# Chunked inverses of an RWKV layer: odd heads written across partition halves, and the series taken by powers

## The chip, the cores and the metric

The kernel runs on one core of one Trainium2 chip. The metric is the device time of one execution in microseconds (us). Besides the trace of one profiled execution there are three timed runs.

## The reference

A transformer of three layers over 512 tokens of width 1024: a window-attention layer, a grouped-attention layer, and a hybrid layer that adds the outputs of a sparse attention and of an RWKV-7 recurrence. The change touches the recurrence alone:

```
def rwkv7_step(state, inp):
    r_t, w_t, k_t, v_t, kk_t, a_t = inp
    sa = jnp.einsum('bhvk,bhk->bhv', state, -kk_t)
    state = (state * w_t[:, :, None, :] + sa[..., None] * (kk_t * a_t)[:, :, None, :]
             + v_t[..., None] * k_t[:, :, None, :])
    y = jnp.einsum('bhvk,bhk->bhv', state, r_t)
    return state, y
```

It has 8 heads of 64 keys by 64 values. After the scan come a group norm, a bonus term, a gate, and the product with `w_out`, whose second half of rows belongs to the recurrence and whose first half to the attention.

## The kernel before

The recurrence isn't stepped token by token. The 512 tokens are 4 tiles of 128 (index `i`), and each tile holds two chunks of 64 tokens: chunk 0 on partitions 0 to 63, chunk 1 on 64 to 127. For each head and chunk the kernel needs the inverse of a 64 x 64 triangular matrix of 1 minus A, where A is made of `grams` (products of the scaled keys) under masks. A is cut in two: its blocks of 16 x 16 on the diagonal (`mA`, and transposed `mD`) and the rest (`mE`). The near part is inverted by a series, then the far part by another series over it. Each step of a series is one **product**: for all 8 heads and both chunks, 16 matmuls of 64 x 64 by 64 x 64 in fp32 (each is two records in the trace). The names are A2, D2, Q2, D4, Z1, Z2, Z3 (near), QT (a transpose), KT, Y1_, Y2_ and RR (far), and X (values). RR is the inverse; `solved` multiplies it into values and decayed keys (HG), `state_maps`, `state_adds`, `own_outputs`, `state_step` and `state_outputs` carry the state, and `mean_job`, `square_job`, `spread_job` are the group norm.

TensorE (PE) writes each job to one of 8 PSUM banks in turn (`begin`), and can't begin a job before the one 8 before it has been copied out. Of one product, chunk 0 goes from partitions 0 to 63 into PSUM partitions 0 to 63, and chunk 1 from 64 to 127 into 64 to 127:

```
for h in range(8):
    for cs in halves_c:
        ins = mm(b[cs, h * CH:h * CH + CH], left[cs, h, :], right[cs, h, :], True, True)
```

So a product uses two of the four 64 x 64 quarters of the array. ScalarE (ACT) or VectorE (DVE) takes it out of PSUM (`move`, `plus`; `plus` adds the identity or the sum so far), and the next product waits for that. Between dependent products the program puts other work by hand, above all pieces of the output product (`out_part`: matmuls of 128 x 128 by 128 x 512, fp32), one at a time.

All orders are written out by hand: PE, ACT, DVE, GpSimd (POOL) and SyncE (SP) each run their own list, and meet at semaphores. In iteration `i` PE does the grams of tile `i` and the inverses of tile `i`, with the state work of tile `i-1` in between. Tile 0 has no earlier tile, and more `out_part` pieces beside it. After tile 3 a tail of state work and output products remains.

At the end of POOL's list stand a wait for four loads and one DMA issue:

```
pool.wait_ge(S("R_ar"), 16)
for i in range(NT):
    pool.wait_ge(s_x[i], 32)
pool.dma_start(gb2[:, :], ...).then_inc(s_gb[1], 16)
```

`s_x[i]` reaches 32 when `x_kept[i]`, the residual stream of tile `i` that was put out to HBM earlier, is back in SBUF (`x_out`). SP issues these four loads one after the other when the last projection of the recurrence is done. `gb2` is the row of final gains. On DVE only the additions to `x_out` (`add_half`) wait for `s_x[i]`, each for its own tile.

Of the kernel before, what the change touches and what calls it, by code (L numbers as in the profile page):

```python
# [25 lines left out]
F32 = mybir.dt.float32  # L26
# [80 lines left out]
def program(nc, A, out):  # L107
    ctx = ExitStack()
    with ctx:
# [30 lines left out]
        bank = [ctx.enter_context(nc.psum_tensor(f"bank{b}", [P, 512], F32)) for b in range(NBANK)]  # L140
# [157 lines left out]
        order, slot, J, who, nth, count = [], {}, {}, {}, {}, {"a": 0, "v": 0}  # L298
# [131 lines left out]
        mixB = hT[:, :, :].rearrange("p (j h) t -> p j h t", h=2)[:, :, 0, :]  # L430
        PC = stat[:, 544:576].rearrange("p (j c) -> p j c", j=4)
# [22 lines left out]
        def _(pe):  # L454
            def begin(key, consumer, apart=False):

                n = len(order)
                if n >= NBANK:
                    evacuated(pe, order[n - NBANK])
                order.append(key)  # L460
                if not apart:
                    opened.append(key)
                slot[key], who[key] = n % NBANK, consumer
                return bank[slot[key]]

            opened = []
# [623 lines left out]

            def product(key, consumer, left, right, after=()):

                for k in after:
                    evacuated(pe, (k, key[1]))
                b = begin(key, consumer)
                for h in range(8):
                    for cs in halves_c:
                        ins = mm(b[cs, h * CH:h * CH + CH], left[cs, h, :], right[cs, h, :], True, True)
                end(ins)

            def grams(i):
# [20 lines left out]
                for j in range(4):  # L1122
                    for c in range(2):
                        t0 = i * P + CH * c
                        for e in range(2):
                            es = slice(64 * e, 64 * e + 64)
                            ins[e] = mm(bs[e][halves_c[c], j * CH:j * CH + CH], AR[es, j, i, 0, CH * c:CH * c + CH],
                                        aF[es, j, t0:t0 + CH], True, True)
# [3 lines left out]
            def solved(i):  # L1132

                for k in (("RR", i), ("X", i), ("tm", i, 1)):
                    evacuated(pe, k)
                for bt in range(2):
                    b = begin(("HG", i, bt), "a")
                    for q in range(4):
                        h = 4 * bt + q
                        for cs in halves_c:  # L1140
                            ins = mm(b[cs, q * P:(q + 1) * P], mT[cs, h, :], XG[cs, h, :], True, True)
                    end(ins)
# [72 lines left out]
            def values(i):  # L1215
# [3 lines left out]
                b = begin(("X", i), "a")  # L1219
                for h in range(8):  # L1220
                    for cs in halves_c:
                        ins = mm(b[cs, h * CH:h * CH + CH], BX[cs, i % 2, h, 2, :], vtm[cs, h * 64:h * 64 + 64], True, True)
                end(ins)

            def turned(i):

                evacuated(pe, ("Z3", i))
                b = begin(("QT", i), "a")
                for h in range(8):
                    for cs in halves_c:  # L1230
                        ins = mm(b[cs, h * CH:h * CH + CH], Qa[cs, h, :], C("ident64")[cs, :], True, True)
                end(ins)
# [3 lines left out]
            def out_part(half, n, i, pieces=4):  # L1236
# [4 lines left out]
                if key not in co:  # L1241
# [3 lines left out]
                    co[key] = (begin(key, "v", apart=True), 0)  # L1245
# [26 lines left out]

            grams(0)
            token_major(0, (2, 3))
            out_part(0, 0, 0, 3)
            pe.wait_ge(S("R_rk"), 4)
            bonus_sums(0)
            values(0)
            bonus_sums(1)
            evacuated(pe, ("gd", 0, 1))  # L1280
            product(("A2", 0), "a", mD, mA)
            product(("D2", 0), "a", mA, mD)
# [3 lines left out]
            pe.wait_ge(S("R_q1"), 1)  # L1286
            product(("Q2", 0), "v", mD2, Qa, ("D2",))
            product(("D4", 0), "a", mA2, mD2)
            out_part(0, 1, 0, 1)
            product(("Z1", 0), "v", mD, Qb, ("D4", "Q2"))  # L1290
            out_part(0, 1, 0, 1)
            product(("Z2", 0), "v", mD, Qa, ("Z1",))
            out_part(0, 1, 0, 1)
            product(("Z3", 0), "v", mD, Qa, ("Z2",))
# [3 lines left out]
            product(("KT", 0), "a", mE, mA2, ("QT",))  # L1298
            out_part(0, 0, 1, 1)
            product(("Y1_", 0), "v", mD, Qa, ("KT",))  # L1300
            out_part(0, 0, 1, 1)
            product(("Y2_", 0), "v", mD, Qb, ("Y1_",))
            token_major(0, (0, 1))
            out_part(0, 0, 1, 1)
            product(("RR", 0), "v", mD, Qb, ("Y2_",))

            for i in range(1, NT):
# [8 lines left out]
                token_major(i, (2, 3))  # L1316
                state_step(p, 0)
                values(i)
                evacuated(pe, ("gd", i, 1))
                product(("A2", i), "a", mD, mA)  # L1320
                product(("D2", i), "a", mA, mD)
                state_step(p, 1)
                pe.wait_ge(S("R_q1"), i + 1)
                product(("Q2", i), "v", mD2, Qa, ("D2",))
                product(("D4", i), "a", mA2, mD2)
# [1554 lines left out]
```

## Time and profile before

| | |
|---|---|
| timed runs, median (lowest, highest) | 1192.81 us (1189.97, 1193.13) |
| profiled execution, its own time | 1190.88 us |
| span of the profile | 1189.1 us |
| PE busy, share of the span | 1130.8 us, 95% |
| DVE, ACT, POOL busy | 596.3, 507.6, 417.3 us |
| mean granted TensorE clock | 0.990 |
| recurrence with its tail, in the span | 1001.3 to 1189.1 |

The span is from the first to the last instruction; the execution's own time is 1.8 us more. PE is busy nearly all the time, but an overlapped, pipelined matmul counts as busy from its start to its modelled end, so what a job costs is read from the distance between the starts of jobs, not from its busy time.

### The profile page before, as it was taken

How to read it: one execution, taken by the hardware profiler on the slowest of the kernel's cores; microseconds unless marked ns; L12 is line 12 of the kernel's file. 1: busy time of each engine (PE TensorE's matmuls, PEld its weight loads, DVE VectorE, ACT ScalarE, POOL GpSimd, SP SyncE). 2: the span in 40 equal slices, each digit the busy share in tenths (PEclk: the TensorE clock that was granted, in tenths of full speed). 3: DMA queues.
4: the chain of work that ended last, by engine and by line, in shares of the span. 5: the costliest groups of instructions: out<-in, count | busy, mean ns of one | idle time of the engine just before them, and what ended most of it. 6: DMA issues, size and time to landing. Idle time of an engine off the chain costs nothing.

```text
span 1189.1 us, 24304 instructions
## 1 busy us (share of the span) xinstructions
PE 1130.8 (95%) x10103; PEld 947.9 (80%) x10103; DVE 596.3 (50%) x1312; ACT 507.6 (43%) x1025; POOL 417.3 (35%) x363
## 2 busy tenths in 40 slices
PE   3999999999999999899999999988999999999996
PEld 3998888799998998656699998966777787677763
DVE  5000001872327347798723439027874897345646
ACT  4232222973424432488824345343884521122221
POOL 4734574776335445400153335230006342000000
PEclk9999999999999999999999999999999999999998
DMA  7432343323222223200042223352002223100001
GB/s 219 148 99 80 106 105 108 99 56 100 72 72 71 92 87 106 71 1 2 1 142 72 72 71 125 107 159 71 2 2 71 71 72 115 55 31 3 4 2 71
DMA packets 73335, 89.57 MB, mean 75 GB/s; under 512 B 2017, under 2 KB 66666, under 8 KB 73098
## 3 DMA queue, kind: packets, MB, share of 16 engines
q1 hardware_dynamic: 70136, 78.12, 20.5%
q0 software_dynamic: 2416, 8.26, 2.9%
q10 hardware_dynamic: 674, 1.64, 0.5%
q8 instruction: 80, 1.31, 0.5%
q14 instruction: 29, 0.24, 0.1%
HBM read 83.75 MB, written 4.26 MB: 74 GB/s over the span
## 4 chain that ended last, share of the span: by engine, by line
PE 83%; DVE 6%; ACT 4%; DMA 2%; POOL 2%; issue 1%; ACTq 1%; DVEq 0%; POOLq 0%
PE bank L477 76%; PE bank L804 2%; POOL ring_parts L2699 2%; ACT arena L1380 1%; PE bank L714 1%; DMA arena<-x_kept 1%; PE bank L1003 1%; ACT ring_parts L1409 1%; PE bank L569 1%; ACT arena L1761 1%; ACT arena L1496 1%; DMA vrow<-in_final_norm_g 1%; DVE arena L2422 0%; ACTq L1375 0%; DMA ring<-in_cmp_w_v 0%
## 5 line engine op out<-in xcount | busy, mean ns | idle before, releaser
L2699 POOL TENSOR_TENSOR ring_parts<-ring,ring_parts 128x512 fp32r<-128x512 f32 (+1 forms) x236 | 308.8, 1341 | 431.7 <-ACT ring_parts L1409 340.7
L477 PE MATMUL bank<-ring_parts,arena_parts 128*128 128x256 f32 x1856 | 322.1, 283 | 0.0
L477 PEld LDWEIGHTS bank<-ring_parts,arena_parts 128*128 128x128 f32 x1856 | 271.4, 190 | 1.7 <-issue 1.3
L477 PE MATMUL bank<-hT_parts,ring_parts 128*128 128x512 f32 x704 | 234.4, 395 | 0.0
L477 PE MATMUL bank<-arena_parts,ring_parts 128*128 128x512 f32 x640 | 223.5, 399 | 2.8 <-POOL ring_parts L2699 2.8
L477 PE MATMUL bank<-ring_parts,hT_parts 128*128 128x256 f32 x1024 | 221.1, 283 | 3.8 <-POOL ring_parts L2699 2.9
L1380 ACT ACTIVATE arena<-bank 128x512 f32<-128x512 f32 (+5 forms) x287 | 135.0, 539 | 191.8 <-PE bank L477 171.0
L477 PEld LDWEIGHTS bank<-ring_parts,hT_parts 128*128 128x128 f32 x1024 | 170.6, 191 | 5.0 <-POOL ring_parts L2699 3.7
L477 PE MATMUL bank<-arena 64*64 64x64 f32 (+7 forms) x1904 | 163.4, 316 | 7.9 <-ACT arena L1761 2.9
L477 PEld LDWEIGHTS bank<-hT_parts,ring_parts 128*128 128x128 f32 x704 | 133.0, 189 | 31.2
L477 PEld LDWEIGHTS bank<-arena_parts,ring_parts 128*128 128x128 f32 x640 | 121.5, 190 | 31.5 <-ACT arena L1380 3.0
L477 PEld LDWEIGHTS bank<-arena 128*64 128x64 f32 (+3 forms) x1904 | 107.6, 147 | 46.5 <-issue 16.2
L1409 ACT ACTIVATE ring_parts<-ring 128x2048 fp32r<-128x2048 f32 (+1 forms) x59 | 111.3, 1886 | 40.6 <-PE bank L477 39.9
L1988 DVE SCALAR_TENSOR_TENSOR arena<-arena,bank 128x512 f32<-128x512 f32 x8 | 5.5, 688 | 172.0 <-ACT arena L1484 172.0
L2716 POOL TENSOR_TENSOR hT_parts<-hT,arena_parts 128x512 fp32r<-128x512 f32 x16 | 20.4, 1287 | 90.8 <-ACT arena_parts L1435 90.7
L477 PE MATMUL bank<-ring,arena 64*64 64x64 f32 (+3 forms) x512 | 49.6, 303 | 1.1 <-DMA ring<-in_cmp_w_v 1.0
L1632 ACT ACTIVATE arena<-bank,stat 128x512 f32<-128x512 f32 x64 | 43.2, 689 | 12.9 <-PE bank L477 6.6
L477 PEld LDWEIGHTS bank<-arena,x 64*64 64x64 f32 x1024 | 35.4, 134 | 15.4 <-DVE arena L2497 9.6
L2055 DVE TENSOR_TENSOR x<-x,bank 128x256 f32<-128x256 f32 x32 | 13.5, 421 | 67.6 <-PE bank L477 67.4
L2196 DVE TENSOR_REDUCE stat<-bank 128x1 f32<-128x512 f32 x64 | 39.7, 683 | 13.1 <-PE bank L477 13.1
L2094 DVE SCALAR_TENSOR_TENSOR arena<-arena,bank 128x256 f32<-128x256 f32 x32 | 13.5, 421 | 62.7 <-PE bank L477 62.7
L1552 ACT ACTIVATE arena<-bank,stat 128x256 f32<-128x256 f32 x32 | 15.2, 476 | 68.6 <-PE bank L477 68.6
(271 smaller groups left out, 1409.9 us busy)
## 6 DMA issues: line engine op xcount, KB each, us to landing
ring<-in_a_w_in SPq DMA_DIRECT2D x16, 1024.0 KB, 5.5
ring<-in_w_in SPq DMA_DIRECT2D x15, 1024.0 KB, 5.5
ring<-in_b_w_in SPq DMA_DIRECT2D x10, 1024.0 KB, 5.0
ring<-in_ple_w_gate SPq DMA_DIRECT2D x8, 1024.0 KB, 5.2
arena<-rpb_rows POOLq DMA_DIRECT2D x16, 256.0 KB, 3.5
ring<-in_a_w_out SPq DMA_DIRECT2D x4, 1024.0 KB, 5.3
ring<-in_b_w_out SPq DMA_DIRECT2D x4, 1024.0 KB, 5.3
ring<-in_w_out SPq DMA_DIRECT2D x4, 1024.0 KB, 5.1
```

The costliest lines, as they stand in the source:

```text
L477: return nc.tensor.matmul(o, l, r, start=start, stop=stop)
L569: ins = nc.tensor.transpose(b[:, i * P:(i + 1) * P], x[:, i, k * P:(k + 1) * P], ident)
L804: ins = nc.tensor.transpose(b[:, k * P:(k + 1) * P], pB[u % 8][:, k * P:(k + 1) * P], ident)
L1380: return nc.scalar.activation(o, i, ACT.Copy, scale=scale)
L1409: nc.scalar.activation(rounded(high_slot(n)[:, 0:m]), raw_slot(n)[:, 0:m], ACT.Copy).then_inc(s_whi, 1)
L1552: give(nc.scalar.activation(thp[:, u % 4, :], b[:, 0:256], ACT.Tanh, scale=ple_half[:, i:i + 1]), key)
L1632: give(nc.scalar.activation(pB[u % 8], b[:, :], ACT.Exp, bias=stat[:, c:c + 1], accum_out=stat[:, c + 8:c + 9]), key)
L2055: give(TT(xs, xs, b[:, 0:w], ALU.add), key)
L2094: give(STT(tp[:, u % 2, :], thp[:, u % 4, :], 1.0, b[:, 0:256], ALU.add, ALU.mult), key)
L2196: nc.vector.tensor_reduce(stat[:, 128 + u % 8:129 + u % 8], b[:, :], X, ALU.max, negate=True)\
L2699: nc.gpsimd.tensor_tensor(rounded(r), r, read_back(high_slot(n)[:, o:o + m // 4]), ALU.subtract)\
L2716: nc.gpsimd.tensor_tensor(rounded(hT[:, j, :]), hT[:, j, :], read_back(o_high[:, T * j:T * j + T]), ALU.subtract)\
```

## The change

It has five parts.

1. **Crossed halves.** In every product the odd heads change halves: what is read on partitions 0 to 63 is written to 64 to 127, and the other way round. Even heads stay. Even heads go to one PSUM bank and odd heads to a second (`begin2`), and the copy out reads both banks in one instruction (`both`). `solved` (HG) is done likewise. So that odd heads' inputs lie in the right half, `grams` writes eight more small matmuls per tile (A of the odd heads, crossed, masked by DVE into `mAo`), and ACT copies the decayed keys in three pieces instead of one (`move_decayed`).
2. **Powers.** The near series is Q2 = (1 + D2)(1 + A), Q3 with 1 + D4, Q4 with 1 + D8, with D2, A2, D4, A4, D8 as squares; the far one is KT, K, K2 (its square), Q5 and RR. A tile has 15 products, before 13.
3. **Sums on POOL.** Three of the additions of the identity, and the first one (1 + A), become four POOL instructions per tile, `plus_one` there, at the end of POOL's list, behind the wait for `s_x` and the DMA shown above. DVE keeps two (`D8`, `K2`), before it had seven and 1 + A. ACT copies the rest, and ACT's copy of A4 waits for `R_q1`, the semaphore of POOL's first addition.
4. **Banks.** Bank 7 is held for `out_part` until tile 3 is done, and all other jobs cycle over 7 banks.
5. **Order.** PE's and ACT's lists are rewritten around the new products; `out_part` pieces in tile 0 from Q2 on remain eight.

```diff
+        def both(key):
+            a, b = slot[key], second_slot[key]
+            return ap(bank[a], [(CH, 4), (512 * (b - a), 2), (1, CH)])
...
+            def begin2(key, consumer):
+
+                if cycle[1] < cycle[0]:
+                    cycle.append(cycle.pop(0))
+                slot[key], who[key] = next_bank(key), consumer
+                second_slot[key] = next_bank(key)
+                return bank[slot[key]], bank[second_slot[key]]
...
+            crossed = ((slice(0, CH), slice(CH, P)), (slice(CH, P), slice(0, CH)))
             def product(key, consumer, left, right, after=()):
 
                 for k in after:
                     evacuated(pe, (k, key[1]))
-                b = begin(key, consumer)
-                for h in range(8):
-                    for cs in halves_c:
-                        ins = mm(b[cs, h * CH:h * CH + CH], left[cs, h, :], right[cs, h, :], True, True)
-                end(ins)
+                even, odd = begin2(key, consumer)
+                for j in range(4):
+                    for here, there in crossed:
+                        o = slice(j * CH, j * CH + CH)
+                        mm(even[here, o], left[0][here, j, :], right[0][here, j, :], True, True)
+                        ins = mm(odd[there, o], left[1][here, j, :], right[1][here, j, :], True, True)
+                end(ins, key)
...
+            cycle.remove(NBANK - 1)
...
+            def second_q(i):
+                pe.wait_ge(S("R_q1"), i + 1)
+                pe.wait_ge(S("R_plus"), 3 * i + 1)
+                product(("Q2", i), "a", heads_i, heads_qa)
...
+            def far_q(i):
+                product(("K2", i), "v", heads_a, heads_d, ("K",))
+                pe.wait_ge(S("R_plus"), 3 * i + 3)
+                product(("Q5", i), "a", heads_i, heads_qb)
...
-                product(("Z1", i), "v", mD, Qb, ("D4", "Q2"))
+                product(("D8", i), "v", heads_a, heads_d, ("A4",))
+                out_part(*late, 1)
+                third_q(i)
                 mean_job(p)
-                product(("Z2", i), "v", mD, Qa, ("Z1",))
-                out_part(*late, 1)
-                product(("Z3", i), "v", mD, Qa, ("Z2",))
+                product(("Q4", i), "a", heads_d2, heads_qa, ("D8", "Q3"))
                 out_part(*late, 1)
                 turned(i)
+                out_part(*late, 1)
+                far(i)
                 square_job(p)
-                product(("KT", i), "a", mE, mA2, ("QT",))
                 out_part(*late, 1)
-                product(("Y1_", i), "v", mD, Qa, ("KT",))
-                out_part(*late, 1)
-                product(("Y2_", i), "v", mD, Qb, ("Y1_",))
+                far_q(i)
                 token_major(i, (0, 1))
-                product(("RR", i), "v", mD, Qb, ("Y2_",))
+                product(("RR", i), "a", heads_d2, heads_qa, ("K2", "Q5"))
                 spread_job(p)
...
+                    move2(("D4", i), mD)
+                    act.wait_ge(S("R_q1"), i + 1)
+                    move2(("A4", i), mA)
...
             pool.dma_start(gb2[:, :], bass.AP(A["final_g_2"].tensor, 0, [[0, P], [1, D]])).then_inc(s_gb[1], 16)
 
+            def plus_one(dst, src, sem):
+                nc.gpsimd.tensor_tensor(dst[:, :, :], src, ap(C("ident64"), [(0, 8), (1, CH)]), ALU.add).then_inc(S(sem), 1)
+
+            for i in range(NT):
+                pool.wait_ge(S("R_gram"), 4 * i + 4)
+                if i:
+                    pool.wait_ge(filled, J[("RR", i - 1)] + 1)
+                plus_one(Qa, mA, "R_q1")
+                evacuated(pool, ("D2", i))
+                plus_one(mI, mD2, "R_plus")
+                evacuated(pool, ("D4", i))
+                plus_one(mJ, mD, "R_plus")
+                evacuated(pool, ("KT", i))
+                plus_one(mI, mD, "R_plus")
```

First place: the end of POOL's list. The names are those of the tiles; `in_final_g` is the source of `gb2`, `x_loaded` are the semaphores `s_x`. Before:

```order
L2699 TENSOR_TENSOR ring_parts_51<-ring,ring_parts_51 128x512 x3
L2699 TENSOR_TENSOR ring_parts_51<-ring,ring_parts_51 128x512 [waits weight_high_parts]
L2699 TENSOR_TENSOR ring_parts_51<-ring,ring_parts_51 128x512 x3
L2818 DMA arena<-in_final_g 128x1024 [waits x_loaded2,x_loaded1,x_loaded3,x_loaded0,R_ar]
L109 UNCONDITIONAL_BRANCH
```

And of the change:

```order
L2765 TENSOR_TENSOR ring_parts_51<-ring,ring_parts_51 128x512 x3
L2884 DMA arena<-in_final_g 128x1024 [waits x_loaded2,x_loaded1,x_loaded3,x_loaded0,R_ar]
L2887 TENSOR_TENSOR arena<-x,cst 128x512 [waits R_gram]
L2887 TENSOR_TENSOR arena<-arena,cst 128x512 [waits drained_by_scalar]
L2887 TENSOR_TENSOR arena<-x,cst 128x512 [waits drained_by_scalar] x2
L2887 TENSOR_TENSOR arena<-x,cst 128x512 [waits filled,R_gram]
```

The last three kinds of rows are new: 1 + A, 1 + D2, then 1 + D4 and 1 + KT of tile 0, and the start of tile 1. They stand behind the DMA that waits for all four loads of `x_kept`.

Second place: PE in tile 0, from the last bonus sum to the transpose of Q. Before, the 64x64 rows are Q2, D4, Z1, Z2, Z3 and the transpose (`cst,arena`), each 1 and 15 matmuls, and the 128x512 rows from `ring,arena` are pieces of `out_part`:

```order
L477 MATMUL bank<-arena 64x64 [waits drained_by_vector,drained_by_scalar,R_q1]
L477 MATMUL bank<-arena 64x64 x15
L477 MATMUL bank<-arena 64x64 [waits drained_by_vector]
L477 MATMUL bank<-arena 64x64 x15
L477 MATMUL bank<-ring,arena 128x512 [waits drained_by_scalar,raw_loaded0]
L477 MATMUL bank<-arena,x 64x64 [waits drained_by_vector,drained_by_scalar]
L477 MATMUL bank<-arena,x 64x64 x15
L477 MATMUL bank<-ring,arena 128x512
```

And of the change, from D4 on; the products are D4, A4, Q2 (the row with `R_q1`), D8 and Q3:

```order
L508 MATMUL banks<-arena 64x64 [waits drained_by_scalar]
L508 MATMUL banks<-arena 64x64 x15
L508 MATMUL banks<-arena 64x64 [waits drained_by_scalar]
L508 MATMUL banks<-arena 64x64 x15
L508 MATMUL banks<-arena 64x64 [waits drained_by_vector,R_plus,R_q1]
L508 MATMUL banks<-arena 64x64 x15
L508 MATMUL banks<-ring,arena 128x512 [waits drained_by_vector,raw_loaded0]
L508 MATMUL banks<-x 64x64 [waits drained_by_scalar]
L508 MATMUL banks<-x 64x64 x15
L508 MATMUL banks<-ring,arena 128x512
L508 MATMUL banks<-arena 64x64 [waits drained_by_scalar,R_plus]
L508 MATMUL banks<-arena 64x64 x15
```

Q2 now waits for two semaphores of POOL, before for one of DVE, and everything behind it on PE, the pieces of `out_part` too, stands behind that wait.

## Rows read from the trace of the kernel before

**Rows 1.** The page: busy time, share of the span, instructions of each engine.

```profile
PE 1130.8 (95%) x10103; PEld 947.9 (80%) x10103; DVE 596.3 (50%) x1312; ACT 507.6 (43%) x1025; POOL 417.3 (35%) x363
```

**Rows 2.** Windows, tile 1 and the tail: length, busy (instructions) of each engine, clock, DMA.

```profile
1037.24:1072.89 35.65, 35.25 (x823) 27.72 (x819) 18.66 (x45) 8.83 (x17) 0.57 (x1) 1.00 0.09 31
...
1144.58:1189.10 44.52, 34.58 (x326) 18.50 (x326) 25.93 (x73) 9.19 (x18) 0.00 (x0) 0.92 0.12 48
```

**Rows 3.** Timeline of PE, tile 0 into tile 1: start, length, operation, records.

```profile
1036.30 1.15 PE L477 MATMUL bank<-arena,x 64*64 64x64 f32 x32
1037.24 2.02 PE L477 MATMUL bank<-hT,arena 64*64 64x128 f32 x64
...
1039.03 0.70 PE L477 MATMUL bank<-arena,hT 64*64 64x64 f32 x32
...
1039.53 1.96 PE L477 MATMUL bank<-arena,x 64*64 64x128 f32 x32
...
1041.42 1.12 PE L477 MATMUL bank<-ring,arena 128*128 128x512 f32 x2
```

**Rows 4.** Timeline of POOL and of SP's queue from 985 on.

```profile
1047.22 0.57 POOL L2818 DMA_DIRECT2D arena<-in_final_g  x1 [59.45 <-DMA arena<-x_kept]
...
1002.32 20.34 SPq L2849 DMA_DIRECT2D arena<-x_kept  x4
```

**Rows 5.** Windows during and after the four loads; the last two columns are DMA share, GB/s.

```profile
1026.00:1046.60 20.60, 20.60 (x388) 14.17 (x392) 10.27 (x21) 3.48 (x6) 0.00 (x0) 1.00 0.13 53
1052.00:1060.00 8.00, 7.72 (x209) 6.62 (x205) 3.89 (x7) 2.34 (x4) 0.00 (x0) 1.00 0.01 2
```

**Rows 6.** Timeline of tile 0 around Q2; in brackets idle time before, and its releaser.

```profile
1016.63 0.69 DVE L2507 TENSOR_TENSOR arena<-arena,bank 128x512 f32<-128x512 f32 x1 [0.61 <-DMA arena<-x_kept]
...
1017.46 2.08 PE L477 MATMUL bank<-arena 64*64 64x64 f32 x64 [1.32 <-DVE arena L2507]
...
1019.48 1.12 PE L477 MATMUL bank<-ring,arena 128*128 128x512 f32 x2
...
1020.53 1.15 PE L477 MATMUL bank<-arena,x 64*64 64x64 f32 x32
...
1021.61 1.12 PE L477 MATMUL bank<-ring,arena 128*128 128x512 f32 x2
1021.73 0.69 DVE L2497 TENSOR_TENSOR arena<-bank,arena 128x512 f32<-128x512 f32 x1 [2.31 <-PE bank L477]
```

**Rows 7.** Groups by line and shape from 960 on (x228: whole program): busy, mean ns.

```profile
L1380 ACT ACTIVATE arena<-bank 128x512 f32<-128x512 f32 x36 | 21.1, 597 | 65.8 <-PE bank L477 47.9 <-PE bank L1212 17.8
...
L2699 POOL TENSOR_TENSOR ring_parts<-ring,ring_parts 128x512 fp32r<-128x512 f32 x228 | 303.2, 1362 | 335.5 <-ACT ring_parts L1409 335.3
...
L2699 POOL TENSOR_TENSOR ring_parts<-ring,ring_parts 128x512 fp32r<-128x512 f32 x11 | 17.6, 1629 | 11.3 <-ACT ring_parts L1409 11.3
...
L1212 PE MATMUL bank<-cst,arena 128*128 128x128 f32 x48 | 6.8, 277 | 0.0
```

**Rows 8.** Timelines of PE and DVE, end of tile 1 and start of tile 2.

```profile
1063.87 1.05 PE L477 MATMUL bank<-cst,arena 128*128 128x2 f32 x8
...
1072.30 0.66 PE L1270 MATMUL bank<-cst,arena 128*128 128x128 f32 x4
...
1064.96 0.17 DVE L2524 TENSOR_SCALAR stat<-bank 128x8 f32<-128x8 f32 x1 [2.42 <-PE bank L477]
...
1067.38 0.43 DVE L2527 COPY arena<-stat 128x512 f32<-128x512 f32 x1
...
1076.46 0.55 DVE L2561 TENSOR_TENSOR ring<-bank,cst 128x384 f32<-128x384 f32 x1
```

**Rows 9.** Timeline of PE near the start of the program.

```profile
25.24 0.80 PE L477 MATMUL bank<-ring_parts,hT_parts 128*128 128x256 f32 x2 [0.40 <-POOL ring_parts L2699]
...
27.97 0.44 PE L477 MATMUL bank<-ring_parts,hT_parts 128*128 128x256 f32 x2
...
29.08 0.40 PE L477 MATMUL bank<-ring_parts,hT_parts 128*128 128x256 f32 x2
```

More of the change, by code:

```diff
@@ L139, in program @@
         arena = sb2("arena", [P, NARENA], (0, 12288), (16384, 9728))
-        bank = [ctx.enter_context(nc.psum_tensor(f"bank{b}", [P, 512], F32)) for b in range(NBANK)]
+        banks = ctx.enter_context(nc.psum_tensor("banks", [P, NBANK, 512], F32))
+        bank = [banks[:, b, :] for b in range(NBANK)]
         x_kept = nc.dram_tensor("x_kept", [NT, P, D], F32, kind="Internal").ap()
@@ L454, in _, with next_bank, begin @@
         def _(pe):
[L455 to L460, printed above, removed]
+            cycle, holds = list(range(NBANK)), {}
+            def next_bank(key, n=None):
+                if n is None:
+                    n = cycle.pop(0)
+                    cycle.append(n)
+                if n in holds:
+                    evacuated(pe, holds[n])
+                holds[n] = key
+                return n
+            def begin(key, consumer, apart=False, n=None):
                 if not apart:
                     opened.append(key)
-                slot[key], who[key] = n % NBANK, consumer
+                slot[key], who[key] = next_bank(key, n), consumer
                 return bank[slot[key]]
+            def begin2(key, consumer):
[4 more added lines that the diff above has]
+                return bank[slot[key]], bank[second_slot[key]]
             opened = []
@@ L1218, in values, with out_part @@
                 evacuated(pe, ("gr", i, 1, 1))
[L1219 to L1223, printed above, removed]
-            def turned(i):
[L1227 to L1232, printed above, removed]
+                product(("X", i), "a", heads_of(BX[:, i % 2, :, 2, :]), heads_of(vtm.rearrange("p (h v) -> p h v", h=8)))
+            def turned(i):
+                evacuated(pe, ("Q4", i))
+                eye = ap(C("ident64"), [(0, 4), (1, CH)])
+                product(("QT", i), "a", heads_of(Qb), (eye, eye))
             co = {}
-            def out_part(half, n, i, pieces=4):
+            def out_part(half, n, i, pieces=4, hold=NBANK - 1):
                 key = ("CO", half, n, i)
@@ L1820, in move, with move2, move_decayed @@
                 give(copy(dst, b[:, :].rearrange("p (h t) -> p h t", h=8)), key)
+            def move2(key, dst):
+                take(act, key)
+                give(copy(by_head(dst), both(key)), key)
+            def move_decayed(i):
+                key = ("tm", i, 0)
+                b = by_head(take(act, key)[:, :].rearrange("p (h t) -> p h t", h=8))
+                d = by_head(XG[:, :, CH:P])
+                copy(d[:, :, 0, :], b[:, :, 0, :])
+                copy(d[0:CH, :, 1, :], b[CH:P, :, 1, :])
+                give(copy(d[CH:P, :, 1, :], b[0:CH, :, 1, :]), key)
             def square_out(i):
@@ L1833, in _ @@
                 if i:
-                    for bt in range(2):
-                        key = ("HG", p, bt)
+                    for e in range(2):
+                        key = ("HG", p, e)
                         b = take(act, key)
-                        give(copy(HG[:, 4 * bt:4 * bt + 4, :], b[:, :].rearrange("p (h t) -> p h t", h=4)), key)
+                        give(copy(by_head(HG)[:, :, e, :], b[:, :].rearrange("p (h t) -> p h t", h=4)), key)
                     for c in range(2):
@@ L2491, in _, with plus_one @@
             nc.vector.memset(Sst[:, 0, :], 0.0).then_inc(S("R_state"), 1)
[L2493 to L2497 removed]
+            def plus_one(key, dst):
+                take(dve, key)
+                give(TT(by_head(dst), both(key), ap(C("ident64"), [(0, 4), (0, 2), (1, CH)]), ALU.add), key)
             def add_half(half, n, i):
```

164 lines of the change are left out of this document (87 added, 77 removed).

## The prediction

> **What bounds the kernel now.** The page first: PE is busy for 95% of the span, the other engines for half of it or less [rows 1]. The windows by tile say the same of the recurrence: tile 1 lasts 35.65 us with PE busy for all but 0.4 us, at granted clock 1.00, which is 2.4 GHz; DVE has 18.7 us of work in it, ACT 8.8, POOL next to none [rows 2]; tiles 2 and 3 give two more such rows. So inside a tile the distance between starts of PE jobs is the price. A product (32 records, two quarters of the array) costs 0.94 us when a job on 64x64 tiles follows (1036.30 to 1037.24), and 1.08 when a 128-wide matmul follows (1020.53 to 1021.61) [rows 3, 6]. Then I looked for jobs that work on all four quarters. The last job of `grams` has also 32 records of 64x64x64, and takes 0.50 us (1039.03 to 1039.53); its 64-wide neighbour HG, on two quarters, takes 1.89 (1039.53 to 1041.42), where `grams`, 64 records of the same shape on four quarters, takes 1.79 for double the matmuls [rows 3]. A product on four quarters should take 0.47, half of 0.94.
>
> Last I asked of each engine that gets new work what stands ahead of it in its own list. POOL's last row decides this case: it sat idle for 59.45 us until a DMA from `x_kept` landed, and issued the gain row at 1047.22 [rows 4]. The four loads were handed over by SP from 1002.32 on, and moved at a steady 53 to 54 GB/s, 13% of the DMA engines, until 1046.6, then nothing more [rows 4, 5]. Before, nobody minds: the gain row is used at the very end.
>
> **The change, step by step.**
>
> *The new wait.* POOL's additions stand behind that wait. Q2 of tile 0 needs two of them. POOL is free at 1047.22 + 0.57 = 1047.79. The trace has no POOL addition of a 128x512 fp32 operand and a constant; with two full operands one takes 1.36 us in the mean of 228, and 1.63 in the mean of the 11 from 960 us on, beside busy DVE work [rows 7]. I take 1.36, since DVE is nearly idle there, and 1.63 as the upper bound; nothing smaller of this size is at hand, and 0.2 less would take 0.4 from the sum. 1 + A is ready at 1049.15, 1 + D2 at 1050.51. PE starts 0.14 after a release (1016.63 + 0.69 to 1017.46) [rows 6], so Q2 starts at 1050.65. PE would get there at about 1016: in the trace it arrives at 1017.46 - 1.32 = 1016.14, and ahead of Q2 the change halves three products (-1.4) and puts D4, A4 and a wider gram job there (+1.4). PE stands for some 34 us. ACT stands too, since its copy of A4 waits for 1 + A, and DVE behind D8.
>
> *Tile 0 from Q2 on.* Before, 1017.46 to 1037.24, 19.78 us, with 10 products and 8 pieces of `out_part`; after, again 10 products and 8 pieces: 19.78 - 10 x 0.47 = 15.1. Is the shorter chain still covered? A link is product 0.73 (0.47 and the 0.26 by which the consumer of the old product started later than 0.94: 1020.53 to 1021.73 is 1.20), copy 0.60 by ACT [rows 7] and 0.14: 1.47 us. PE has product and piece between: 1.08 - 0.47 and 1.05 (1019.48 to 1020.53), which is 1.66. Yes, by 0.2. Tile 1 starts at 1050.65 + 15.1 = 1065.75 instead of 1037.24 [rows 3]: **+28.5 us**.
>
> *Tiles 1 to 3.* Products: 13 x 0.94 before, 15 x 0.47 after, -5.2. HG on four quarters: 1.89 to 0.95, -0.9. The last gram job: 16 matmuls become 24, of which row half 1 gets two thirds, so 0.50 to 0.94, +0.4. PE before also waits here about 0.8 per tile for D2 and for the copy of the values, which the new order does away with (rows 2 show at least 0.4 of it). Together -6.5. Two new waits come back, both on DVE. (a) RR waits for K2's addition. `spread_of` runs on DVE from 1064.96 to 1067.81, starting 1.1 after its PE job at 1063.87 [rows 8]; behind it come `add_half` and K2, 0.6 and 0.69 [rows 6]: 1.1 + 2.85 + 0.6 + 0.69 + 0.14 = 5.4 after that PE job, in which PE has 0.98 (`square_job`), 1.05 (a piece), 0.47 + 0.61 (K2, Q5) and 1.1 (two jobs of transposes, 8 records at 6.8 / 48 [rows 7]): 4.2. Wait 1.2. (b) With 7 banks the grams take six and HG one, and its second bank is that of the first gram, so HG waits for DVE's masks. From `spread_job` at 1072.30 to the end of that mask at 1077.01 are 4.71 us [rows 8], all of it DVE finishing the tile before; PE has 0.6 (to 1072.89 [rows 2]), 1.8 and 0.94 = 3.3 of work in it. Wait 1.5, in tiles 2 and 3 only. Before, HG had a bank and started at once [rows 3]. So -5.3, -3.8, -3.8: **-12.9**. POOL's later additions are hidden: tile 1 starts after 1065, and three of them and the chain leave POOL idle for most of a tile.
>
> *Tail*: HG again, **-0.9**; the rest of its 44.5 us [rows 2] is as it was. ACT's `move_decayed` and the banks lie beside PE work.
>
> *The clock.* After a pause PE has begun slowly in this trace: from 25.24 to 27.97 12 records take 2.73 us (0.23 each), from 27.97 to 29.08 nine take 1.11 (0.12 each) [rows 9], the levels of 1.2 and 2.4 GHz. A pause of 34 us is of that kind; I pay 2.9 us at half rate once, **+1.5** (nothing at the least).
>
> Sum: 28.5 - 12.9 - 0.9 + 1.5 = +16.2 on this execution's own 1190.88: 1207.1. The median of the three runs, 1192.81, is 1.9 above the profiled one, so 1209.0. Forecast **1209**.
>
> *A rule against the change.* Rows 3 show four quarters at work at once with the two quarters of one row half under way together, though there issued two apart, not as neighbours like in the new product. The Trainium skill, "TensorE: Matmul & The Clock Gate", Part 3, says that a weight load overlaps matmuls in flight only if its row group differs. By that rule neighbours on one row half would take turns. The 0.50 us of the gram job, which has row halves in common too, speaks against it here.
>
> **The rivals.**
>
> 1. *Row halves conflict; a product stays at 0.94.* Then +10 x 0.47 in tile 0, and + 15 x 0.47 + 0.95 in each of three tiles, +0.9 in the tail: +29.6, less some 3 of the DVE waits that PE then covers: 1236. For it: no job in the trace has this issue order. Against: 0.50 against 0.94 [rows 3]. Chance 0.05. The Trainium skill's rule above is this rival.
> 2. *The clock stays at 1.2 GHz long after the pause.* PE's jobs in tile 0 would take double for the rest of the tile, +15: 1223. For: the work after the pause is broken by waits. Against: the recurrence runs at 1.00 throughout with the same kind of work [rows 2]. Chance 0.04.
> 3. *Faster: POOL gets past its wait early.* Were the loads of `x_kept` back by about 1016, Q2 wouldn't wait: no 34.5 and no 1.5, which gives 1209 - 36 = 1173. The sign turns where POOL gets through at 1047.2 - 16.2 = 1031.0. For: the loads are issued at 1002 and the DMA engines are 87% idle. Against: the rate was the same in both halves of the 44 us, so it is the loads' own [rows 5], and nothing in the change touches them. Chance 0.04.
> 4. *The gain comes out smaller or larger, near no change*: that needs 16 us more of savings in three tiles. 0.01.
>
> The forecast has 0.86. Its own range: below, no clock price (-1.5) and half of the DVE waits absent (-3.5), 1204; above, POOL additions at 1.63 (+1), products at 0.55 instead of 0.47 as the gram job's 0.50 hints (+4), +1.5 for the clock again, 1216. The rivals together hold 0.14, so the range 1203 to 1216 needs none of them. A measurement of this kernel tells some 0.3% (3.6 us) from no change. Faster 0.04, same 0.01, slower 0.95.
>
> **What would show it.** In the profile after: PE idle for about 34 us in tile 0 ahead of a 64x64 job, the waits naming POOL's addition, and that one a DMA from `x_kept`; POOL's first addition at about 1047.8, tile 1 about 1066; products of 32 records 0.47 to 0.50 apart; tiles 1 to 3 30.4, 31.9 and 32.2 long; waits of 1.2 before RR and 1.5 before HG on DVE; a low clock only after the pause. The prediction is wrong if POOL's first addition starts long before 1047, if products stay near 0.94 apart, or if a tile of the rest is as long as before.

## The result, and the profile after

The changed kernel takes 1217.36 us in the median of three runs (1215.47 to 1221.56), the kernel before 1192.81: a ratio of 1.0217, 95% interval 1.0195 to 1.0240. It is slower, as forecast, but by 24.6 us and not by 16.2, just above the range that was given. The profiled execution is the 1221.56 one.

The page of the changed kernel: each engine's busy time, and PE's granted clock in 40 slices of the span:

```profile
PE 1117.6 (92%) x10423; PEld 932.9 (76%) x10423; DVE 578.3 (47%) x1292; ACT 524.2 (43%) x1061; POOL 433.9 (36%) x379
...
PEclk9999999999999999999999999999999997699998
```

PE is busy for 13 us less than before, in a span that is 31 us longer [rows 1]: PE works less and stands more. Where it stands shows in the windows of the recurrence (start and end, length, busy and instructions of each engine, clock, DMA share, GB/s), tile 0, tiles 1 to 3, and the tail:

```profile
1004.93:1071.79 66.86, 31.78 (x641) 19.01 (x642) 13.69 (x27) 10.17 (x19) 4.86 (x5) 0.72 0.15 56
1071.79:1105.84 34.05, 30.14 (x907) 22.53 (x898) 14.64 (x40) 13.54 (x28) 4.35 (x4) 1.00 0.01 3
1105.84:1141.92 36.08, 31.23 (x895) 23.71 (x895) 16.80 (x45) 13.07 (x27) 4.37 (x4) 0.95 0.01 4
1141.92:1176.10 34.18, 30.00 (x895) 22.44 (x894) 16.85 (x46) 13.28 (x27) 4.36 (x4) 1.00 0.01 3
1176.10:1219.80 43.70, 33.73 (x326) 17.65 (x326) 26.00 (x73) 9.07 (x18) 0.00 (x0) 0.93 0.13 49
```

Before, tile 0 took 35.91, tile 1 35.65, the three tiles together 107.34 (1144.58 - 1037.24) and the tail 44.52 [rows 2, 3]. Now tile 0 takes 31 more, tiles 1 to 3 together 104.31, which is only 3.0 less, and the tail 0.8 less. The code ahead of the recurrence is the same, and its end scatters from run to run: in the other traces of this case it lies between 1000.1 and 1002.8, here at 1004.9.

The pause of tile 0, from the timeline of all engines:

```profile
1050.98 0.58 POOL L2884 DMA_DIRECT2D arena<-in_final_g  x1 [59.62 <-DMA arena<-x_kept]
1051.58 1.11 POOL L2887 TENSOR_TENSOR arena<-x,cst 128x512 f32<-128x512 f32 x1
1052.63 1.10 POOL L2887 TENSOR_TENSOR arena<-arena,cst 128x512 f32<-128x512 f32 x1
1052.72 0.60 ACT L1436 ACTIVATE x<-banks 128x512 f32<-128x512 f32 x1 [32.94 <-POOL arena L2887]
...
1053.83 1.13 PE L508 MATMUL banks<-arena 64*64 64x64 f32 x32 [34.24 <-issue]
1054.89 2.07 PE L508 MATMUL banks<-ring,arena 128*128 128x512 f32 x2
...
1058.10 0.69 DVE L2574 TENSOR_TENSOR arena<-banks,cst 128x512 f32<-128x512 f32 x1 [37.01 <-PE banks L508]
...
1059.96 0.69 PE L508 MATMUL banks<-arena 64*64 64x64 f32 x32
1060.59 1.12 PE L508 MATMUL banks<-ring,arena 128*128 128x512 f32 x2
```

POOL stands 59.62 for `x_kept` as before (59.45 [rows 4]), and now three engines stand behind it: PE 34.24, ACT 32.94, DVE 37.01. PE's wait is labelled "issue" although it is one on POOL's semaphores: POOL's second addition, 1 + D2, ends at 1052.63 + 1.10 = 1053.73, and PE starts 0.10 later. Then the clock: two records of 512 columns take 2.07 at 1054.89 and 1.12 at 1060.59, so the clock is at its lower level until 1059.96. From Q2 to tile 1 are 17.96 us.

The timeline of PE in tile 1 has something that the prediction did not. These are all the rows from 1070 to 1092, and two of 1103 to 1111, that have idle time before them:

```profile
1083.08 0.46 PE L508 MATMUL banks<-ring,arena 64*64 64x64 f32 x10 [0.92 <-issue]
1087.04 0.34 PE L508 MATMUL banks<-arena,ring 64*64 64x64 f32 x5 [0.48 <-issue]
1090.74 0.80 PE L508 MATMUL banks<-arena 64*64 64x64 f32 x21 [1.26 <-issue]
1104.63 0.69 PE L508 MATMUL banks<-arena 64*64 64x64 f32 x32 [1.25 <-DVE arena L2574]
1110.08 1.10 PE L508 MATMUL banks<-arena,x 64*64 64x128 f32 x32 [1.22 <-DVE ring L2638]
```

The last two are RR waiting for K2's addition and HG for the masks, foreseen at 1.2 and 1.5. The first three stand in the middle of jobs, where PE has no semaphore to wait for. Tiles 2 and 3 have one each, of 2.4 and 1.6. The DMA view of 1080 to 1092, in 40 slices of 0.3 us, shows what else goes on there:

```profile
GB/s 0 0 55 0 0 0 0 0 0 0 0 0 0 0 55 0 0 0 0 0 0 0 0 0 0 0 0 0 55 0 0 0 0 0 0 0 0 0 0 0
...
q8 instruction: 3, 0.05, 1.6%
```

Three packets of an instruction queue, 16 KB each, at about 1080.7, 1084.3 and 1088.5: each 2.3 to 2.7 ahead of a resumption. The three together take 1.6% of 16 engines in 12 us, about 1 us of one engine each. That suggested that PE had run out of instructions.

### The profile page after: what moved, and what is told of

The parts are those of the page before. It is cut to its first block, busy times and chain, and to the rows that moved or that the text cites. A ratio compares the mean times of both kernels' runs of the same rounds, so it can differ in the third digit from the quotient of the medians.

```text
span 1219.8 us, 25014 instructions
## 1 busy us (share of the span) xinstructions
PE 1117.6 (92%) x10423; PEld 932.9 (76%) x10423; DVE 578.3 (47%) x1292; ACT 524.2 (43%) x1061; POOL 433.9 (36%) x379
## 3 DMA queue, kind: packets, MB, share of 16 engines
q10 hardware_dynamic: 674, 1.64, 0.5%
q8 instruction: 83, 1.36, 0.5%
## 4 chain that ended last, share of the span: by engine, by line
PE 79%; DVE 7%; ACT 4%; DMA 3%; issue 2%; POOL 2%; SPq 1%; ACTq 1%; DVEq 0%; POOLq 0%
PE banks L508 72%; DMA arena<-x_kept 3%; PE banks L835 2%; POOL ring_parts L2765 1%; PE banks L745 1%; PE banks L1034 1%; ACT arena L1436 1%; SPq L2930 1%; ACT ring_parts L1465 1%; PE banks L600 1%; ACT arena L1552 1%; ACT arena L1817 1%; ACTq L1431 1%; DVE arena L2500 0%; ACT arena L1445 0%
## 5 line engine op out<-in xcount | busy, mean ns | idle before, releaser
L508 PE MATMUL banks<-ring_parts,arena_parts 128*128 128x256 f32 x1856 | 322.4, 283 | 0.0
L508 PEld LDWEIGHTS banks<-ring_parts,arena_parts 128*128 128x128 f32 x1856 | 271.9, 190 | 2.3 <-DVE stat L2325 1.5
L508 PE MATMUL banks<-hT_parts,ring_parts 128*128 128x512 f32 x704 | 235.6, 396 | 0.0
L508 PE MATMUL banks<-arena_parts,ring_parts 128*128 128x512 f32 x640 | 225.1, 402 | 2.8 <-POOL ring_parts L2765 2.8
L508 PE MATMUL banks<-ring_parts,hT_parts 128*128 128x256 f32 x1024 | 222.6, 285 | 3.8 <-POOL ring_parts L2765 2.9
L1436 ACT ACTIVATE arena<-banks 128x512 f32<-128x512 f32 (+6 forms) x311 | 145.4, 535 | 187.4 <-PE banks L508 182.9
L508 PE MATMUL banks<-arena 64*64 64x64 f32 (+6 forms) x2544 | 173.5, 295 | 48.4 <-issue 39.5
L508 PEld LDWEIGHTS banks<-ring_parts,hT_parts 128*128 128x128 f32 x1024 | 171.8, 192 | 5.0 <-POOL ring_parts L2765 3.7
L508 PEld LDWEIGHTS banks<-hT_parts,ring_parts 128*128 128x128 f32 x704 | 133.5, 190 | 31.1
L508 PEld LDWEIGHTS banks<-arena_parts,ring_parts 128*128 128x128 f32 x640 | 122.9, 192 | 32.2 <-ACT arena L1436 3.1
L1688 ACT ACTIVATE arena<-banks,stat 128x512 f32<-128x512 f32 x64 | 43.1, 688 | 12.9 <-PE banks L508 6.7
L1608 ACT ACTIVATE arena<-banks,stat 128x256 f32<-128x256 f32 x32 | 15.2, 474 | 68.6 <-PE banks L508 68.6
```

What stands on the lines that cost most here:

```text
L508: return nc.tensor.matmul(o, l, r, start=start, stop=stop)
L1436: return nc.scalar.activation(o, i, ACT.Copy, scale=scale)
L1608: give(nc.scalar.activation(thp[:, u % 4, :], b[:, 0:256], ACT.Tanh, scale=ple_half[:, i:i + 1]), key)
L1688: give(nc.scalar.activation(pB[u % 8], b[:, :], ACT.Exp, bias=stat[:, c:c + 1], accum_out=stat[:, c + 8:c + 9]), key)
```

## The experiments

Two theories on the cost. *First*: the pause and the low clock behind it are the slowdown, four quarters do pay, and some of the pay is lost to the fetching of PE's instructions. *Rivals*: the powers are the longer chain; four quarters pay nothing; the gaps belong to banks or operands. The runs fall into three groups, each with the kernel before on the same chip: 1190.7 us beside the unblocked, two-quarter, filled and reordered ones, 1191.5 beside the shifted, warm, spread and repeated ones, 1194.9 beside the last bench.

**The pause taken away.** In POOL's list the gain row and its waits for the four loads go behind the additions:

```diff
-            for i in range(NT):
-                pool.wait_ge(s_x[i], 32)
-            pool.dma_start(gb2[:, :], ...)
             for i in range(NT):
                 ... the additions ...
+            for i in range(NT):
+                pool.wait_ge(s_x[i], 32)
+            pool.dma_start(gb2[:, :], ...)
```

> The changed kernel with POOL's gain row, and the waits for the four x_kept loads ahead of it, moved behind POOL's additions; nothing else. The additions then wait for their own inputs alone. If the slowdown is PE's pause of 34.2 us ahead of Q2 in tile 0 and the half clock after it (about 3 us), this kernel is at 1217.4 - 34.2 - 3 = 1180 us (1177 to 1184), faster than the kernel before, with no low clock in tile 0. If the powers themselves are too long a chain (more products and additions behind each other), the pause is replaced by shorter waits in tile 0 and the time stays above 1195. If the pause doesn't come from POOL's place in line, nothing changes: 1217.

Measured: 1179.96 (1178.61 to 1182.09), ratio 0.991 (0.9892 to 0.9928), faster than before by 10.8 us. The windows of its tiles 1 and 2:

```profile
1033.35:1067.62 34.27, 30.15 (x908) 22.54 (x899) 14.65 (x40) 13.55 (x28) 4.37 (x4) 1.00 0.07 25
1067.62:1101.85 34.23, 30.02 (x895) 22.43 (x894) 16.80 (x45) 13.11 (x27) 4.38 (x4) 1.00 0.02 4
```

Tile 0 shrinks from 66.86 to 30.98 (1002.37 to 1033.35), with no low clock; the other tiles stay as in the changed kernel. The pause with its clock is 36 to 37 us (1216.34 in the changed kernel's second run, or 1217.36, less 1179.96), the whole of the slowdown and more. The chain of powers does not set the time: no tile is longer than before.

**Two quarters again.** The unblocked kernel, the odd heads' results in the other half:

```diff
-                        ins = mm(odd[there, o], left[1][here, j, :], ...)
+                        ins = mm(odd[here, o], left[1][here, j, :], ...)
```

> As the unblocked one, but the odd heads' half of every product goes into the partition half that it came from, so that a product uses two quarters of the array again (the same number of instructions; the values of the odd heads are wrong from there on, so only its time is read). If four quarters are what pays, each of the 60 products takes 0.94 instead of 0.47: +28 us, less about 8 for the gaps inside dense jobs, which disappear if they come from PE's instruction blocks (128 matmul records then last 3.75 us, not 1.9), and about 2 for waits on DVE that PE then covers: 18 above the unblocked one, 1198 (1193 to 1208). If tiles are set by the chain of copies and additions and not by PE, it stays within 4 us of the unblocked one. If the gaps come from banks or semaphores, they stay and the difference is 26 or more.

Measured: 1198.02 (1196.95 to 1198.76), ratio 1.006 (1.0044 to 1.0076), 18.1 above the unblocked one. From 1000 on, PE waits for "issue" once in it, 0.9 us, against six times and 6.1 us in the unblocked kernel. So powers whose products don't cross cost 7 (HG and the gram job still cross in it), and crossing gives back 18. Each product gives back 0.30 us of its 0.47 (18.1 / 60). Of the 10 us between 60 x 0.47 and 18.1, the lists of PE's waits show 9.6 in the unblocked kernel that aren't in this one: 5.2 for "issue", 2.9 for K2's addition (3.8 against 0.9), and 1.5 for the additions to `x_out` (1.8 against 0.3).

**The pause as a bench.** The changed kernel, blocked, with overwritten products in the pause:

```diff
             def second_q(i):
+                if i == 0:
+                    for n in range(44):
+                        for j in range(4):
+                            for here, there in crossed:
+                                mm(even[here, o], ...)
+                                mm(odd[there, o] if n < 24 else even[here, 256 + ...], ...)
```

> The changed kernel as it is, blocked as it is, with 44 extra products whose results are overwritten in PE's pause ahead of Q2 of tile 0: 24 that cross (four quarters), then 20 that don't (two quarters), about 30 us in all at 0.47 and 0.94, a whole number of 128-record blocks. Two questions. Clock: if the half clock after the pause costs 3 us, this is at 1214.4 with a granted clock near 1 from 1048 to 1060; if it costs nothing, 1217.4. Gaps: if PE's instruction fetch is what leaves gaps in dense jobs, the crossing part runs at 2.3 to 2.6 us for each 128 records after the first few, with a gap about every 125 records and an instruction block's DMA 2.3 to 2.7 ahead of each resumption, and the other part at 3.75 without gaps. If the gaps come from banks, operands or semaphores, neither part has gaps, and 128 crossing records last 1.9 us throughout.

Measured: 1219.70 (1218.96 to 1220.63), ratio 1.0243 (1.0223 to 1.0263). PE's rows with idle time, five of the crossing part, then two of the other, and the windows of most of both parts:

```profile
1019.15 2.09 PE L508 MATMUL banks<-arena,ring 64*64 64x64 f32 x128 [0.83 <-issue]
1022.89 2.10 PE L508 MATMUL banks<-arena,ring 64*64 64x64 f32 x128 [1.64 <-issue]
1026.62 2.10 PE L508 MATMUL banks<-arena,ring 64*64 64x64 f32 x128 [1.64 <-issue]
1030.36 2.09 PE L508 MATMUL banks<-arena,ring 64*64 64x64 f32 x128 [1.64 <-issue]
1033.81 2.33 PE L508 MATMUL banks<-arena,ring 64*64 64x64 f32 x128 [1.36 <-issue]
1037.55 15.18 PE L508 MATMUL banks<-arena,ring 64*64 64x64 f32 x512 [1.41 <-issue]
1053.11 3.31 PE L508 MATMUL banks<-arena,ring 64*64 64x64 f32 x106 [0.38 <-issue]
```

```profile
1019.15:1037.55 18.40, 10.71 (x641) 10.03 (x641) 0.00 (x0) 0.00 (x0) 0.00 (x0) 1.00 0.15 57
1037.55:1052.50 14.95, 14.95 (x511) 14.95 (x512) 0.00 (x0) 0.60 (x1) 3.78 (x4) 1.00 0.21 70
```

This is the clearest reading of the case. Crossing products come in runs of exactly 128 records and then a gap: 640 records in 18.40, or 3.68 for 128. Products on two quarters take 14.95 for 512, or 3.74 for 128, with no gap inside them and one of 0.38 behind them; in the run with the warm pause, below, 1024 of them have none at all. **Back to back, products of 64 columns are no faster on four quarters than on two.** The expectation had 2.3 to 2.6 for each 128 and was too low. The four loads of `x_kept` were under way during the crossing part (57 GB/s), but they are not what sets its pace: in tile 1 of the changed kernel's second run, at 4 GB/s, gaps end at 1080.55, 1084.23 and 1088.20, 3.68 and 3.97 apart. The DMA view of 1019 to 1038 counts five packets of the instruction queue for five runs; a matmul record has its weight load beside it, so 128 records are 256 instructions:

```profile
q8 instruction: 5, 0.08, 2.0%
```

On the clock, the time can't be read as planned, since the crossing part took twice what I had counted on. POOL's second addition ended at 1050.36 in this run, but the filling kept PE until about 1056.7 (a product's 0.63 ahead of the piece at 1057.36), some 6.3 us longer. From there to tile 1 (1071.92) are 15.2 us, with the clock at 1.00 from 1054 to 1060, where the changed kernel needs 17.96 or, in its second run, 17.66: the low clock costs 2.5 to 2.8. The times agree: 6.3 later, less 2.5 to 2.8, is 3.5 to 3.8 more, and 1219.70 is 3.4 above 1216.34.

**Shifted by half a block.** Two extra products on two quarters in the same place.

> The changed kernel as it is, with 64 extra 64x64 matmul records (two products on two quarters, overwritten) in PE's pause of tile 0, where they cost nothing. They push everything behind them by 64 records, half an instruction block. If the gaps inside dense jobs of tiles 1 to 3 belong to the blocks of PE's instructions, they move by 64 records and sit in other jobs (before: 1083.08, 1087.04, 1090.74, 1125.06, 1160.24). If they belong to the jobs, their operands or their banks, they stay at the same jobs.

One run, 1220.12. PE's rows with the longest gaps in tiles 1, 2 and 3, and windows from the start of the program to two of them:

```profile
1085.71 1.84 PE L508 MATMUL banks<-arena 64*64 64x64 f32 x83 [1.96 <-issue]
...
1120.11 2.11 PE L508 MATMUL banks<-arena 64*64 64x64 f32 x100 [1.64 <-issue]
1123.99 0.35 PE L508 MATMUL banks<-x 64*64 64x64 f32 x9 [1.32 <-issue]
...
1155.59 2.34 PE L508 MATMUL banks<-arena 64*64 64x64 f32 x116 [1.71 <-issue]
```

```profile
0.00:1085.71 1085.71, 1005.66 (x7968) 856.78 (x7968) 516.27 (x1111) 481.58 (x977) 424.55 (x370) 0.98 0.26 80
0.00:1120.11 1120.11, 1035.93 (x8847) 879.35 (x8848) 533.07 (x1156) 493.94 (x1002) 427.82 (x373) 0.98 0.26 78
```

The same rows and windows of the unshifted kernel, run again (1216.34, 1213.87 to 1218.04):

```profile
1088.20 0.80 PE L508 MATMUL banks<-arena 64*64 64x64 f32 x21 [1.53 <-issue]
...
1121.98 1.15 PE L508 MATMUL banks<-arena 64*64 64x64 f32 x36 [1.82 <-issue]
...
1155.77 1.38 PE L508 MATMUL banks<-arena 64*64 64x64 f32 x52 [1.61 <-issue]
```

```profile
0.00:1088.20 1088.20, 1005.94 (x7967) 857.02 (x7968) 514.08 (x1111) 483.09 (x979) 424.87 (x370) 0.97 0.26 80
...
0.00:1121.98 1121.98, 1035.43 (x8846) 879.03 (x8847) 530.88 (x1156) 495.56 (x1004) 429.24 (x374) 0.98 0.25 78
```

PE stops after record 7967 or 7968 and after 8846 or 8847 in both, though 64 more records stand ahead. So each gap sits 64 records earlier in its job: the records of that job left behind it are 83, 100 and 116 in the shifted kernel, 21, 36 and 52 in the other. (In the first pair the difference is 62; some records can be missing from a trace.) The gaps belong to the place in the instruction stream. Of the unshifted kernel's second run, whose ratio was 1.0206 (1.0185 to 1.0227), this was expected:

> The changed kernel once more, unchanged, as the base of the comparisons on this chip: 1.022 of the kernel before, 1213 to 1221.

**Long matmuls and wide ones.** The bench once more: 24 crossing products with a matmul of 512 columns behind every second, then 8 crossing products of 128 columns.

> The changed kernel as it is, its pause of tile 0 filled with overwritten work of two kinds. First 24 crossing products with one matmul of 512 columns behind every second one: 768 records of 64 columns and 24 of 512. Then 8 crossing products with 128 columns instead of 64, 256 records. The filled pause with crossing products alone ran at 3.73 us for each 128 records, 22.4 for 24 products, with gaps of 1.86. If a block of 128 records can't be passed in less than 3.7 us and longer matmuls use that time up, the first part takes about 23.1 us (792 records) with gaps of 0.3 or less, the 12 long matmuls coming free; if the gaps are a price of the crossing products themselves, it is 22.4 + 12 x 0.95 = 33.8. The second part runs at 0.94 for each product, 3.7 us for each 128 records, all four quarters at work and no gap; if the gaps belong to four quarters, it has them too.

One run, 1213.42. Windows of the two parts:

```profile
1015.59:1041.36 25.77, 25.77 (x793) 15.86 (x793) 0.69 (x1) 0.00 (x0) 0.00 (x0) 1.00 0.15 57
1041.36:1048.50 7.14, 7.14 (x257) 6.97 (x256) 0.00 (x0) 0.06 (x1) 1.78 (x3) 1.00 0.14 53
```

PE is busy in all of both. At the bench's 3.68 for 128 records 24 crossing products alone take 22.1, so the 12 long matmuls add 3.7 us, not 12; my 23.1 was too low because two products and a long matmul take 2.15 by themselves, 4.2 for 128 records, which is already more than the fetch. The wide products keep four quarters at work without a gap, 7.14 for 257 records: a record does twice the work there. That is 3.56 for 128, a little under the 3.68 of the bench, but only over two blocks. So neither crossing nor four quarters are at fault, but short instructions.

**A warm pause.** 32 extra products on two quarters in the pause.

> The changed kernel as it is, with 32 extra products on two quarters (8 whole instruction blocks, overwritten) in PE's pause: 32 x 0.94 = 30 us, from about 1019 to 1049, so that they end ahead of the release at 1053.8 and PE is at work until shortly before. If the pause costs the clock as well, the granted clock stays at 1.00 from 1054 to 1060, Q2 to the start of tile 1 takes 15.0 instead of 18.0, and the time is 3 us below the changed kernel on the same chip (0.9975 of it). If the clock costs nothing, they are the same.

Measured: 1215.79 (1215.15 to 1216.60), ratio 1.0203 (1.0186 to 1.0221), against 1.0206 for the changed kernel beside it: no difference. The expectation missed, and the rows say why:

```profile
1015.82 30.08 PE L508 MATMUL banks<-arena,ring 64*64 64x64 f32 x1024
1050.37 1.13 PE L508 MATMUL banks<-arena 64*64 64x64 f32 x32 [4.48 <-issue]
1051.44 2.07 PE L508 MATMUL banks<-ring,arena 128*128 128x512 f32 x2
```

The filling ended at 1045.9, PE stood 4.48 us, and that was enough: the clock was at its lower level again, and Q2 to tile 1 took 17.7, as in the changed kernel's second run. A pause of 4.5 costs the clock as much as one of 34. Where the pause was under 1 us (the two benches above), it cost nothing.

**DVE's two waits, and long matmuls into the dense stretch.** On top of the unblocked kernel, the masks ahead of the last steps of the tile before, and K2's addition ahead of the last piece's:

```diff
                 masks(i)
+                if p:
+                    finish_rest(p - 1); gate(p - 1); bonus(p)
...
                 spread_of(p)
-                add_half(*late)
                 plus_one(("K2", i), mD2)
+                add_half(*late)
```

> The unblocked kernel with DVE's two waits taken down: the masks of a tile stand ahead of the last steps of the tile before (four scalings, gate, bonus), and the last piece of out_part goes between Q5 and the transposes, with K2's addition ahead of that piece's own addition on DVE. If HG's wait of 1.44 us (twice) and RR's of 1.5 us (three times) are as the trace says and nothing else comes last right behind them, this is 2.9 + 3 x 0.6 to 3 x 1.0, about 5 us, below the unblocked one: 1175. If the chain behind them is as late, no more than 1 us comes out of it.

Measured: 1177.10 (1175.07 to 1179.91), ratio 0.9886 (0.9867 to 0.9906). From the start of the recurrence to the tail it takes 131.9 (1002.53 to 1134.42) against 133.5 (1002.37 to 1135.83): 1.6, not 5; by the medians the gain is 2.9. HG's wait is gone and RR's is down to 0.7, but what leads the waits of PE in the recurrence has grown:

```profile
PE banks L508 <- issue: 7.5, 7, 1.9
```

against 6.1 in the unblocked kernel. And in tile 3 the clock fell for a moment behind a gap of 1.89 (0.95 in the mean of the tile): the 338 records from there to RR keep PE busy for 14.79, at 1.00 in the changed kernel for 13.23. That is 1.6 us of the time of this trace, which is also the slowest of its five runs. PE came sooner to where it had to wait for its next block; that this is why the gaps grew is not shown. Then two of the four early pieces of `out_part` were moved behind the values and behind A4:

> The kernel with POOL unblocked and DVE reordered, and two of the four early pieces of out_part (4 records of 512 columns, 1.9 us) moved out of the row of four behind HG into the dense stretch: one behind the product of the values, one behind A4. If the gaps come from fetching instructions while PE runs through 128 short records faster than a block arrives, long instructions placed there cost nothing up to the length of the gap (1.7 to 2.1 in each of the three tiles): 1177.1 - 3 x 1.7 = 1172. If the gaps have another cause, the moved pieces only change places and it stays at 1177.

Measured: 1174.34 (1173.28 to 1177.67), ratio 0.9862 (0.9840 to 0.9883). From recurrence start to tail 128.8 (1000.08 to 1128.90), 3.1 less, where 5.1 was expected; the waits:

```profile
PE banks L508 <- issue: 3.8, 6, 1.0
```

The gaps halve, from 7.5 to 3.8, by moving work into them and changing nothing else. The time follows less surely: the clock stays at 1.00 in tiles 1 to 3 of this trace, which is 1.6 of the 3.1, a moved piece isn't free (PE is busy for 30.78 in tile 2, against 29.78 without the move), and the medians differ by 2.8 with overlapping intervals. It is the best of all versions, 17 us ahead of the kernel before on the same chip.

## Why the prediction was half right

- *The pause*: right. POOL free at 1051.56, Q2 48.9 after the recurrence's start, forecast 49.3. POOL's additions take 1.09, not 1.36. (The upper end of the range counts +1 for two additions of 1.63; two times 0.27 is +0.5. Nothing hangs on it.)
- *Tile 0 from Q2 on*: 15.1 was right to 0.1 where the clock stayed up. "I pay 2.9 us at half rate once, +1.5" was mis-sized: it costs 2.5 to 2.8, since PE was slow for 6 us (1053.83 to 1059.96). Tile 0 as a whole is +30.6 in the trace of the second run of the changed kernel, +30.0 forecast; that it comes so near is partly luck, since Q2 was 0.5 early there and the clock cost 1.1 more.
- *Four quarters*: 128 records of crossing products take 2.10 to the end of the last (row at 1022.89), four products; with the last record's own length off, about 0.47 for each, as forecast, so rival 1 falls. The Trainium skill ("TensorE: Matmul & The Clock Gate", Part 3) has a weight load overlap matmuls in flight only if the row group differs. The trace disagrees with that for this order of issue: neighbours share a row half, which by my reading of the rule would have kept a product at 0.94. The same part also lets a load into the "background weight buffer" go ahead, which would fit; no run here tells.
- *DVE's new waits*: nearly right, 1.25 idle before RR and 1.22 before HG. The forecast of 1.2 and 1.5 was made from starts, though, and the idle time begins only at the end of the last record; with its 0.28 and 0.22 they are 1.5 and 1.4, or 7.5 in three tiles instead of 6.6.
- *The tail*: right, -0.8 for -0.9.
- **What failed** is the term "Products: 13 x 0.94 before, 15 x 0.47 after" in tiles 1 to 3, and with it "-12.9". The single product has that length. But a dense stretch of them can't be run through at that rate: in a run of such blocks, 128 records that last under 3.7 us leave PE without instructions for the rest. Before, four products took 3.76, so it could not show there. Measured was -5.0 (second run: 34.03, 34.13, 34.22; before 107.34) or -3.0 (first run, where the clock also fell to 0.95 in tile 2). PE's waits for "issue" in that second run, less the pause, are 6.1 us, most of the 7.9 that are missing. The other 1.8 are covered by an estimate: each of the five gaps costs 0.22 more than its idle time, for the same reason as above (in the bench 3.74 from start to start, less 1.88 for four products, is 1.86, where the row has 1.64), which is 1.1, and DVE's waits are 0.9 longer than forecast.
- The account on the second trace: start +1.5, tile 0 +30.6, tiles -5.0, tail -0.9, together +26.2, the difference of the spans (1215.3 and 1189.1). The forecast was +16.2: 7.9 of the difference is in tiles 1 to 3, 0.6 in tile 0, and 1.5 in the start, which no part of the change touches.
- *Rival 3*, the sign: taking the wait away does make the kernel faster, but at 1180 and not at 1173; 6.1 of the 7 us between are the gaps.

That the gaps are instruction fetch is shown by their place in the stream, their period of 256 instructions, the packets ahead of each resumption, and by long matmuls that fill them. Why one block takes 3.7 us, when its packet takes about 1, is open.

## What to carry to other kernels

Before giving an idle engine work, read what it is waiting for: a wait that costs nothing today becomes the bound of everything put behind it, and here moving one load of a row that is needed at the end changed the verdict from 2.1% slower to 0.9% faster. When making short matmuls faster, count instructions as well as columns: a stretch of several blocks in which PE gets through each 256 instructions (128 matmuls with their loads) in less than some 3.7 us won't get faster, so put long matmuls between them or make them wider. A gap within a job, with no semaphore, is looked up by its distance in records from the next one.

## What the hardware showed that I had not expected

- PE's instructions come in blocks of 16 KB (q8: 5 packets, 0.08 MB), and in a run of five blocks each took 3.68 us (640 records in 18.40), though PE could have passed one in 1.9. The Trainium skill ("Runtime: NRT & Kernel Launch", Instruction fetch mechanics) says that the sequencer fetches blocks of 256 instructions through a queue of its own while it executes, and that crossing a boundary is "mostly hidden". The trace agrees with the block; hidden it was where a block lasted 3.7 us or more (and for two blocks of 3.56), else PE stood for up to 2.4 us.
- After a pause of 4.48 us PE ran at the lower clock level just as after 34.2, until 6.1 us after its restart in the changed kernel; after pauses under 1 us it didn't. Between them it went both ways. Behind a gap of 2.37 in tile 2 of the changed kernel the granted clock was 0.50 from 1125.06 to 1128, and it fell behind one of 1.89 (the kernel with DVE reordered) too, but not behind one of 1.96 (the shifted kernel).
